# Moving the rotary key products of a two-block transformer kernel in between the rank products

## The reference, cut to what matters

```python
h = rmsnorm(x, g_attn[l]) * (1 + sc1) + sh1          # 256 tokens
hc = rmsnorm(xc, g_attn[l]) * (1 + csc1) + csh1      # 256 context tokens
cq, ckv, kr, qn, kn, vn, f = split_columns(h @ w_in[l])        # 512, 512, 64, 512, 512, 512, 512 columns
cq_c, ckv_c, kr_c, qn_c, kn_c, vn_c, f_c = split_columns(hc @ w_in[l])
```

## Time and profile before

| what | us |
|---|---|
| median of 3 runs | 2605.36 |
| lowest and highest run | 2604.16, 2605.70 |
| span of the profiled execution | 2602.8 |
| TensorE busy in that span | 2578.5 |
| VectorE busy | 1763.1 |
| ScalarE busy | 1217.6 |

### The profile page before, as it was taken

One profiled execution on the slowest core, in us unless ns is written; L12 is line 12 of the kernel. 1 busy time (PEld: TensorE's weight loads), 2 busy tenths in 40 slices (PEclk: granted clock), 3 DMA queues, 4 the chain that ended last, 5 costly groups with the idle time before them and its releaser, 6 DMA issues.

```text
span 2602.8 us, 36329 instructions
## 1 busy us (share of the span) xinstructions
PE 2578.5 (99%) x14852; PEld 2212.9 (85%) x14852; DVE 1763.1 (68%) x2432; ACT 1217.6 (47%) x1602; POOL 33.4 (1%) x30
## 2 busy tenths in 40 slices
PE   8999999999999999999999999999999999999998
PEld 5788778888888888888888888899888888888887
DVE  3377977898888877555656677676766666665444
ACT  4442444455555555444433555545544444444443
POOL 2100000000000000000000000000000000000000
PEclk9999999999999999999999999999999999999999
DMA  9887975677777655555555544465555555555554
GB/s 392 352 308 267 334 249 174 220 247 233 239 238 236 208 191 183 196 190 191 184 190 189 169 140 137 156 194 188 188 190 189 189 190 193 187 188 199 194 194 139
DMA packets 151414, 548.72 MB, mean 211 GB/s; under 512 B 16976, under 2 KB 18896, under 8 KB 150352
## 3 DMA queue, kind: packets, MB, share of 16 engines
q1 hardware_dynamic: 148464, 540.34, 61.4%
q10 hardware_dynamic: 2784, 6.06, 0.8%
HBM read 543.72 MB, written 2.10 MB: 210 GB/s over the span
## 4 chain that ended last, share of the span: by engine, by line
PE 95%; DVE 3%; DMA 1%; ACT 1%; issue 0%; SPq 0%; ACTq 0%; DVEq 0%
PE ps L485 42%; PE ps L484 21%; PE ps L497 5%; PE ps L496 5%; PE ps L495 5%; PE ps L489 3%; PE ps L482 3%; PE ps L491 3%; PE ps L490 3%; PE ps L483 1%; DVE raw L448 1%; PE ps L1783 1%; PE ps L2005 1%; DVE lo L437 1%; PE ps L1974 1%; DMA raw_deep<-in_stream 0%
## 5 line engine op out<-in xcount | busy, mean ns | idle before, releaser
L437 DVE TENSOR_TENSOR lo<-raw,hi 128x1024 fp32r<-128x1024 f32 x815 | 993.1, 1223 | 714.6 <-ACT hi L424 712.5
L485 PE MATMUL ps<-pair,hi 128*128 128x512 f32 x3994 | 1390.8, 392 | 0.0
L424 ACT ACTIVATE hi<-raw 128x1024 fp32r<-128x1024 f32 x815 | 860.4, 1059 | 1056.0 <-PE ps L485 763.9
L484 PE MATMUL ps<-pair,lo 128*128 128x256 f32 x3994 | 1119.4, 280 | 0.0
L485 PEld LDWEIGHTS ps<-pair,hi 128*128 128x128 f32 x3994 | 749.9, 188 | 161.1
L484 PEld LDWEIGHTS ps<-pair,lo 128*128 128x128 f32 x3994 | 750.0, 188 | 6.3 <-issue 2.7
L485 PE MATMUL ps<-hid,hi 128*128 128x512 f32 x688 | 238.7, 392 | 0.0
L484 PE MATMUL ps<-hid,lo 128*128 128x256 f32 x688 | 192.3, 280 | 0.0
L1332 DVE TENSOR_REDUCE tmp<-ps 128x256 f32<-128x512 f32 x244 | 165.5, 683 | 0.4
L485 PEld LDWEIGHTS ps<-hid,hi 128*128 128x128 f32 x688 | 129.1, 188 | 28.4
L448 DVE CUSTOM_DVE_ANT_0 raw<-raw,c_bc 128x1024 f32<-128x1024 f32 x128 | 152.9, 1218 | 0.0
(11 more groups left out here) (360 smaller groups left out, 2575.9 us busy)
## 6 DMA issues: line engine op xcount, KB each, us to landing
raw<-in_stream SPq DMA_DIRECT2D x983, 512.0 KB, 4.1
raw_deep<-in_stream SPq DMA_DIRECT2D x31, 512.0 KB, 10.8
xc<-in_xc SPq DMA_DIRECT2D x4, 1024.0 KB, 8.1
x<-in_x ACTq DMA_DIRECT2D x1, 2048.0 KB, 9.1
c_bc<-in_c_bc SPq DMA_DIRECT2D x1, 1024.0 KB, 10.4
bias<-in_rpb ACTq DMA_DIRECT2D x4, 256.0 KB, 4.5
g_bc<-in_g_bc ACTq DMA_DIRECT2D x1, 1024.0 KB, 4.8
out<-out_sb SPq DMA_DIRECT2D x4, 256.0 KB, 2.7
```

Source lines behind the costliest of these rows:

```text
L424: e.activation(hi[:, c % R, :], raw_of(p), ACT.Copy).then_inc(hi_ready, 1)
L437: e.tensor_tensor(lo[:, c % R, :], raw_of(p), hi[:, c % R, :].bitcast(F32), ALU.subtract)\
L484: e.matmul(out[:, T:2 * T], wlo, act[:, 0, :], start=False, stop=False)
L485: return e.matmul(out, whi, both_, start=False, stop=last)
```

## The change

The rotary weights become one full chunk, loaded behind the chunks of feature tile 2 and split once, by two ScalarE and two VectorE instructions, into a place of their own (`krw_hi`, `krw_lo`, in the room of `x`). The product of one feature tile, three matmuls of 512 columns, follows the rank products of a tile from `kt` = 4 on; three more tiles go ahead of `first(15)` and one behind it. The sums are kept in bank 7 instead of 6; the turned modulation rows go into bank 6 behind the rows, and so the first `modulate` matmul of a tile waits for VectorE's reading of the tile before (`mod_ready`). `kn`, `vn` and the statistics take other banks. The two tables are issued behind the last `a` chunk.

```diff
-_stage("a", KT - 1)
-CHUNKS += [("kr", 0), ("a", KT - 1), ("kr", 1)]
+_stage("a", KT)
...
     SEQ.extend(("mod", 4 * _kt + _i) for _i in range(4))
     if LAG - 1 <= _kt:
         SEQ.append(("weights", _kt - LAG + 1))
+    if _kt == 2:
+        SEQ.append(("rotary", 0))
...
+        krw_hi, _ = place("krw_hi", [P, KT, 2, ROPE], F32R, home)
+        krw_lo, _ = place("krw_lo", [P, KT, 2, ROPE], F32R, home + 8 * K1)
...
+        def rotary_hi(e):
+            p = POS[("rotary", 0)]
+            e.wait_ge(landed[PLACE[p]], 16 * NTH[p])
+            src = raw_of(p).rearrange("p (k n) -> p k n", n=ROPE)
+            e.activation(krw_hi[:, :, 0], src, ACT.Copy)
+            e.activation(krw_hi[:, :, 1], src, ACT.Copy).then_inc(krw_hi_ready, 1)
+
+        def rotary_lo(e):
+            src = raw_of(POS[("rotary", 0)]).rearrange("p (k n) -> p k n", n=ROPE)
+            e.wait_ge(krw_hi_ready, 1)
+            e.tensor_tensor(krw_lo[:, :, 0], src, krw_hi[:, :, 0].bitcast(F32), ALU.subtract)
+            e.tensor_tensor(krw_lo[:, :, 1], src, krw_hi[:, :, 1].bitcast(F32), ALU.subtract).then_inc(krw_lo_ready, 1)
...
             e.dma_start(vecs[:], vecs_d).then_inc(s_vecs, 16)
-            for p in range(4, 48):
+            for p in range(4, N_DEEP):
                 load(p)
             e.wait_ge(sqx_sum, 1)
             e.dma_start(c_bc[:], c_bc_d).then_inc(s_cbc_rope, 16)
             e.dma_start(rope[:], rope_tab).then_inc(s_cbc_rope, 16)
-            for p in range(48, len(SEQ)):
+            for p in range(N_DEEP, len(SEQ)):
                 load(p)
...
                 first_hi(kt)
+                if kt == 2:
+                    rotary_hi(e)
...
-            e.wait_ge(weights_used, AT[("kr", 1)] + 1)
+            e.wait_ge(kr_done, 1)
             e.wait_ge(xc_lo, KT)
-            e.activation(tmp[:, 0, :], half(6, 0), ACT.Copy).then_inc(kr_copied, 1)
-            e.activation(tmp[:, 3, :], half(6, 1), ACT.Copy).then_inc(kr_copied, 1)
+            e.activation(tmp[:, 0, :], half(7, 0), ACT.Copy).then_inc(kr_copied, 1)
+            e.activation(tmp[:, 3, :], half(7, 1), ACT.Copy).then_inc(kr_copied, 1)
...
                 first_lo(kt)
+                if kt == 2:
+                    rotary_lo(e)
...
                 if i == 0 and kt:
                     e.wait_ge(mod_rows, kt)
+                    e.wait_ge(mod_ready, kt)
...
-                    r = e.matmul(ps[:, 7, 2 * m:2 * m + 2], mrows[:, kt % 2, m * P:(m + 1) * P], pick, start=True,
+                    r = e.matmul(ps[:, 6, 2 * P + 2 * m:2 * P + 2 * m + 2], mrows[:, kt % 2, m * P:(m + 1) * P], pick, start=True,
                                  stop=True)
...
-            def rotary(i):
-                c = AT[("kr", i)]
-                e.wait_ge(lo_ready, c + 1)
-                if i == 0:
-                    e.wait_ge(mod_rows, KT)
-                for k in range(8):
-                    r = in_both(8 * i + k, 6, split_view(hi, c, 8, P)[:, k], split_view(lo, c, 8, P)[:, k])
-                r.then_inc(weights_used, 1)
+            def rotary(kt):
+                if kt == 0:
+                    e.wait_ge(krw_lo_ready, 1)
+                r = in_both(kt, 7, krw_hi[:, kt].rearrange("p j n -> p (j n)"), krw_lo[:, kt].rearrange("p j n -> p (j n)"))
+                if kt == KT - 1:
+                    r.then_inc(kr_done, 1)
...
                 first(kt - 1, range(3))
                 turn_mod(kt)
                 first(kt - 1, range(3, 8))
-            rotary(0)
+                if kt >= KR_BEHIND:
+                    rotary(kt - KR_BEHIND)
+            for kt in range(KT - KR_BEHIND, KT - 1):
+                rotary(kt)
             first(KT - 1)
-            rotary(1)
+            rotary(KT - 1)
...
-                    r = in_both(kt, (7, 0, 1, 2)[m], whi[:, w], wlo[:, w])
+                    r = in_both(kt, (6, 0, 1, 2)[m], whi[:, w], wlo[:, w])
...
-                    r = tokens(e, ps[:, 3 + tt, :], whi, wlo, a[:, 0], a[:, 1], first_, last)
+                    r = tokens(e, ps[:, (3, 4, 5, 7)[tt], :], whi, wlo, a[:, 0], a[:, 1], first_, last)
...
-                            if g == 0:
-                                e.wait_ge(c_std, 1 + m)
+                            if g == 0 and m == 0:
+                                e.wait_ge(vn_copied, 4)
+                            elif g == 0:
+                                e.wait_ge(c_std, 2)
```

More of the change, by code:

```diff
@@ L23 @@
 LAG = 1
+KR_BEHIND = 4
 DEEP = 4
@@ L360, in two_blocks @@
         rope_hi, qr_moved = sem("rope_hi"), sem("qr_moved")
+        krw_hi_ready, krw_lo_ready, kr_done = sem("krw_hi_ready"), sem("krw_lo_ready"), sem("kr_done")
         kn_copied, vn_copied = sem("kn_copied"), sem("vn_copied")
@@ L417, in split_hi @@
                     e.wait_ge(weights_used, c - R + 1)
[L418 to L424, removed]
+                e.activation(hi[:, c % R, :], raw_of(p), ACT.Copy).then_inc(hi_ready, 1)
         def split_lo(e, a, b):
@@ L429, in split_lo @@
                 e.wait_ge(hi_ready, c + 1)
[L430 to L438, removed]
+                e.tensor_tensor(lo[:, c % R, :], raw_of(p), hi[:, c % R, :].bitcast(F32), ALU.subtract)\
+                    .then_inc(lo_ready, 1)
                 for i in range(FIRST_EXTRA[c], FIRST_EXTRA[c] + EXTRA.get(c, 0)):
                     late_dot(e, i)
+        def rotary_hi(e):
[9 more added lines that the diff above has]
+            e.tensor_tensor(krw_lo[:, :, 1], src, krw_hi[:, :, 1].bitcast(F32), ALU.subtract).then_inc(krw_lo_ready, 1)
         def late_dot(e, i):
@@ L532, in load @@
                         e.wait_ge(lo_ready, i + 1)
+                    elif kind == "rotary":
+                        e.wait_ge(krw_lo_ready, 1)
                     else:
                         e.wait_ge(extra_used, i + 1)
[L535 to L538, removed]
+                e.dma_start(raw_of(p), stream[p]).then_inc(landed[PLACE[p]], 16)
             for i in range(4):
@@ L780, in _ @@
             for m in range(4):
-                e.activation(kn[:, m], by_two(ps[:, (7, 0, 1, 2)[m], :]), ACT.Copy).then_inc(kn_copied, 1)
+                e.activation(kn[:, m], by_two(ps[:, (6, 0, 1, 2)[m], :]), ACT.Copy).then_inc(kn_copied, 1)
             at = upto(at, "vn", 5)
             e.wait_ge(c_stat, 1)
-            e.activation(std[:], half(7, 0), ACT.Sqrt, bias=vec("eps"), scale=1.0 / RANK).then_inc(c_std, 1)
+            e.activation(std[:], half(6, 0), ACT.Sqrt, bias=vec("eps"), scale=1.0 / RANK).then_inc(c_std, 1)
             e.wait_ge(c_stat, 2)
@@ L795, in _ @@
             for tt in range(4):
-                e.activation(vn[:, tt, :], ps[:, 3 + tt, :], ACT.Copy).then_inc(vn_copied, 1)
+                e.activation(vn[:, tt, :], ps[:, (3, 4, 5, 7)[tt], :], ACT.Copy).then_inc(vn_copied, 1)
             for r in range(NA_ROWS):
@@ L1169, in modulation @@
                 e.wait_ge(mod_turned, kt + 1)
-                e.tensor_tensor(first_mod[:, kt], ps[:, 7, 0:4], vec("b_first", 4 * kt, 4), ALU.add).then_inc(mod_ready, 1)
+                e.tensor_tensor(first_mod[:, kt], ps[:, 6, 2 * P:2 * P + 4], vec("b_first", 4 * kt, 4), ALU.add).then_inc(mod_ready, 1)
                 e.wait_ge(mod_ready, kt + 1)
@@ L1883, in statistics @@
                     for m in range(2):
-                        r = e.matmul(half(7, 0), ones, sq_acc[:, 0, m], start=(m == 0), stop=(m == 1))
+                        r = e.matmul(half(6, 0), ones, sq_acc[:, 0, m], start=(m == 0), stop=(m == 1))
                     r.then_inc(c_stat, 1)
@@ L2467, in lay_stream @@
             continue
+        if kind == "rotary":
+            out[p] = rows(w_in, 0, KT, (2 * RANK, 2 * RANK + ROPE))
+            continue
         s, i = (kind, i) if kind == "mod" else CHUNKS[i]
@@ L2473, in lay_stream @@
             out[p] = rows(w_in, i, 1, (0, 2 * RANK))
-        elif s == "kr":
-            out[p, :, 0:CH // 2] = rows(w_in, 8 * i, 8, (1024, 1024 + ROPE))
         elif s in ("qn", "kn", "vn", "f"):
```

## The result

| | before | changed |
|---|---|---|
| median of 21 runs | 2605.16 us | 2609.07 us |
| lowest and highest | 2603.56, 2607.58 | 2606.91, 2610.97 |
| span of the profiled execution | 2602.8 us | 2607.3 us |

The ratio is 1.0015, with a 95% interval from 1.0009 to 1.0021: 3.9 us slower (2.3 to 5.5). The median lies inside the prediction's whole range (2604.4 to 2611.0), 0.4 us beyond the range that had 68% (2606 to 2608.7), and the difference, 0.15%, is within 0.2%.

The account below looks back on a forecast made before the run. TensorE was taken as the bound. Tables -0.7 us and waits +2.6 us summed to +1.9 us on the 2602.8 us span; with 2.5 us from span to median, 2607.2 us (68%: 2606 to 2608.7; whole range 2604.4 to 2611.0).

Parts of the forecast that it names:

- TensorE is the bound, work only moves: Front stage: TensorE is always busy; rotary matmuls take 11.2 us before and after, and shifts run through to the end.
- The tables: Issuing both tables behind the last `a` chunk removes `modulate`'s wait at 82.33 us: -0.7 us.
- the old wait: In the kernel before, `modulate` at 82.33 us waits for the chunk behind the tables, 0.55 us idle; forecast to go.
- Missing cover behind `first(15)`: With one rotary product there, TensorE waits in `kn` 0 (1.13, 0.53, 0.23 us) and at `kn` 2 (0.7): +2.6 us.
- The new wait: `modulate(1)` waits for VectorE's read of `first_mod`; work behind it done at 27.3 us, ahead of `first(0)` at 28.23: cost 0.
- Rival 3: TensorE's clock falls to half speed at `modulate(1)`'s wait: +3.8 us in sum, 2609.2 us; chance 6%.
- The extra chunk: 0.5 MB, 1.3 us, goes ahead of the `mod` chunks of tiles 3 and 4: cost 0, bound 0.7 us.
- The split of the rotary weights: ScalarE and VectorE copies near tile 3 delay `split_lo(3)` by 0.9 us: cost 0, cover 0.3 us, bound 1 us.

Follow-up runs that it names:

- e9: Changed kernel with five fillers ahead of tile 1's `modulate` loop, the wait and the loop's four fillers kept: 2607.46 us, ratio 1.0011.
- e1: Kernel before with one part of the change alone, the two tables issued behind the last rank chunk: 2603.97 us, ratio 0.9997.
- e7: Changed kernel with the two tables put back behind the 48th load: 2608.31 us, ratio 1.0015.
- e4: Kernel of e3 with five rotary products instead of one behind `first(15)`: 2604.20 us, ratio 0.9996.
- e6: Changed kernel with five rotary products instead of one behind `first(15)`, the new wait left in: 2607.27 us, ratio 1.0007.
- e10: Changed kernel with five fillers ahead of tile 1's `modulate` loop and the four inside it removed, the wait kept: 2607.36 us, ratio 1.0010.
- e3: Changed kernel with the first four tiles' turned rows back in bank 7, so `modulate(1)` needs no wait for VectorE: 2606.99 us, ratio 1.0009.
- e8: Kernel of e4 with the rotary chunk loaded and split behind tile 4 instead of tile 2: 2604.07 us, ratio 0.9996.
- e11: Changed kernel with the four fillers taken out of tile 1's `modulate` loop, none put ahead of the wait: 2607.52 us, ratio 1.0010.
- e2: Kernel before with only the new wait added, first `modulate` matmul waiting for VectorE's reading of the tile before: 2606.82 us, ratio 1.0007.
- e5: Changed kernel with ten fillers ahead of the new wait, which stays: 2609.01 us, ratio 1.0016.

## Why the prediction was right, and where it wasn't

The time lay inside the range and the difference within 0.2%, as forecast, but only 1.9 us of the 3.9 are in the sum; the other 2 us came from a step priced at 0. Point by point:

- **TensorE is the bound, work only moves.** Right: the 1.41 us between e9 and the changed kernel at `first(0)` are 1.40 at `kn` 2, and the 4.33 us at `kn` 2 are 4.40 at 306 us.
- **The tables, -0.7 us.** Right in e1 (-0.67). In the changed kernel the old wait is gone as well, but e7 shows that the tables' place has no part in it: the term came out right for another reason than the one given.
- **Missing cover behind `first(15)`, +2.6 us.** Right: 2.5 us. `kn` 2 begins 159.21 - 144.75 = 14.46 us behind E, the end of `first(15)`, where 14.5 was forecast. Without a wait it would be one rotary product, 0.70 us, and the 48 matmuls that take 11.25 us in e4: 11.95 us. In the timeline the waits are 147.24 - 146.15 = 1.09 us for bank 0 (TensorE is done with `kn` 0's part in bank 6 at 144.75 + 1.40), 148.46 - 147.94 = 0.52 for bank 1, 149.40 - 149.16 = 0.24 for bank 2, and the rest, some 0.6 us, ahead of `kn` 2. The view of the waits shows only those of 1.2 and 0.4 us, since it counts from the modelled end of a matmul. e4 and e6 remove them with five products instead of one.
- **The new wait, 0.** This is the step that failed: "Behind it on TensorE stand its 16 matmuls and four fillers, 2.8 us, done at 27.3, ahead of `first(0)` at 28.23." The working of the 2.8 is not written out; 1.86 us for the matmuls and 0.23 for each filler give it. A filler is two instructions, 0.456 us, and in the loop the parts don't run at the speed of an unbroken row: from a chunk to its filler it is 0.57 us and from the filler to the next chunk 0.63. At full speed the loop takes 4.5 us (e9: from 24.63 to 29.14 us). From 24.6 us on it can't be done by 28.23. So even at full clock the wait costs 0.9 us. In e10, where no filler stands in the loop, it takes 2.6 us (24.43 to 27.05) and the wait costs nothing. The trace of before had the answer. There the loop ran at full clock from 22.70 to 27.81 us, paced in part by the landing of its chunks, and the last row has TensorE idle for only 0.41 us ahead of `first(0)`:

```profile
22.70 0.64 PE L1783 MATMUL ps<-raw,csil 128*32 128x256 f32 x8 [0.57 <-DMA raw<-in_stream]
...
27.11 0.70 PE L1774 MATMUL ps<-base 128*128 128x256 f32 x2
```

A start 1.9 us later has only these 0.4 us and the 0.6 us of pacing (5.1 less 4.5) to hide in; 0.9 us is left, as in e9.
- **Rival 3, the clock falls at the new wait.** It was given 6%, and its mechanism came: the granted clock was 0.54 behind the wait. The median lies at this rival's 2609.2 us, which is luck in part, because two terms were off in opposite directions. What was held against it, that matmuls behind an idle stretch of 1.2 us ran at full speed, was from half the idle time, and the windows of the earlier trace rows begin at 46.6 us, so neither could carry the weight. In the changed kernel the low clock ends by 27.8 us and not after 5.8 us, and costs 1.4 us instead of 1.9; the late start adds the 0.9 us that this rival didn't have either.
- **The extra chunk, 0 with a bound of 0.7 us.** The bound: 0.63 us in e3 and 0.64 in e4, gone in e8. In the changed kernel it was hidden behind the 2.4 us.
- **The split of the rotary weights, 0.** Right: between 29 and 236 us the changed kernel has no wait of TensorE for it.

Sum at `kn` 2 in the profile: +2.3 (tile 1), -0.7 (the old wait gone), +2.5 (cover) = +4.1, measured +4.33; the 0.2 us between them is in no wait of the view and stays open. The runs' medians say +3.9.

## What to carry to other kernels

When work is taken out of a row that is never idle, ask what it was covering, not what it cost: 21 matmuls moved ahead of `first(15)` cost nothing themselves, and the list on two other engines that they had covered came out at full length. A wait is only free if everything queued behind it still fits at its measured length, loop and fillers included; read that length from the timeline, and the room from the idle time ahead of the next consumer (0.41 us here). And fillers that are to keep TensorE's clock up must stand where the idle stretch is, ahead of the wait (e10); behind it they did not keep the clock up, and they lengthened the loop (e11 without them is 0.9 us better).

## What the runs showed of the hardware

- Round an idle stretch of TensorE of 2.4 us the clock fell in each of the five kernels that have it: from 24.6 to 28.0 us it was 0.54 (changed kernel), 0.55 (e6), 0.50 (e2), 0.71 (e7) and 0.63 (e11), and a chunk of `modulate`, eight instructions, took 1.08 us instead of 0.64. With 2.3 us of fillers in that stretch (e9, e10) it took 0.64. Neither the fall nor the return came at the same time in each. In e2 the clock was low already from 23.0 us, 1 us into the stretch; in e7 and e11 the first chunk behind it still took 0.64, and the clock fell at 26.0 and 25.5 us. At 28.70 us a chunk took 1.08 in e2 and at 28.44 us 0.64 in the changed kernel; in e11 the clock was low until 32 us. So the cost differs from kernel to kernel: 1.4 us in the changed kernel is what its profile shows, not a constant. The Trainium skill, "TensorE: Matmul & The Clock Gate", Part 1, has the throttled clock as the default that only activity releases. By that rule an idle stretch can bring the low clock back; the traces agree that it does (five of five), and show that the fall can come later than the first work behind the stretch (e7, e11).
- A matmul with fp32 operands and 256 columns (the filler) stands in the trace as two instructions, 0.456 us for both at full clock (e5: 4.56 us for ten), against 0.234 us for one fp32r matmul of 512 columns.
- With a delay of 2.3 us in front, a later wait of 0.63 us could not be seen (the chunk at tile 3); it appeared when the first was mended.
